# The mixer stage of a two-block transformer kernel: input norm applied after the projection, group norm taken in two halves, and the memory rows given a place of their own

## The reference, cut to what matters

```python
hn = _rmsnorm(x, norm_mix[l])                       # x: 256 x 1024
z = hn @ w_in[l]                                    # 1024 x 2560
x_lru, gate, q, k, v = jnp.split(z, splits, axis=-1)  # five parts of 512
y_a = _rg_lru(x_lru, conv_w, conv_b, ...) * jax.nn.gelu(gate)
y_b = _chunk_attention(q, k, v, rel_bias[l])        # 8 heads of 64, band mask and bias
y = jnp.concatenate([_rmsnorm(y_a, norm_grp_a[l]), _rmsnorm(y_b, norm_grp_b[l])], axis=-1)
x = x + y @ w_out[l]                                # 1024 x 1024
x = x + _memory_cross_attention(_rmsnorm(x, norm_cross[l]), _rmsnorm(mem, norm_mem[l]), ...)
```

## Time and profile before

| | us |
|---|---|
| median of 3 runs | 1633.67 (1632.15 to 1634.11) |
| the profiled execution | 1634.35 |
| its span, first to last instruction | 1632.6 |
| TensorE busy | 1527.7 (94%) |
| VectorE busy | 903.1 (55%) |
| ScalarE busy | 818.9 (50%) |
| GpSimd busy | 566.8 (35%) |

### The profile page before, as it was taken

How to read it: one execution, slowest core, us unless ns; L and a number is a source line. 1 busy time by engine, 2 the same in 40 slices (tenths; PEclk the granted TensorE clock), 3 DMA queues, 4 the chain that set the end, 5 groups by cost and what they waited for, 6 DMA issues and landing times.

```text
span 1632.6 us, 28309 instructions
## 1 busy us (share of the span) xinstructions
PE 1527.7 (94%) x10643; PEld 1407.4 (86%) x10643; DVE 903.1 (55%) x2131; ACT 818.9 (50%) x1437; POOL 566.8 (35%) x256
## 2 busy tenths in 40 slices
PE   6999999989979879898999889999999999999998
PEld 5998899978869779888999668999999999999886
DVE  6835348388342332132896996555555555555555
ACT  4546454488335724444455665444444444444444
POOL 5761655510456446726688991000000000000000
PEclk9999999999989979999999999999999999999999
DMA  6750334600233243424254004555554555555553
GB/s 258 278 173 36 142 117 168 220 27 2 101 106 129 78 155 130 155 109 146 81 198 140 1 0 180 181 181 188 191 184 180 181 188 191 184 180 182 176 195 129
DMA packets 37529, 238.47 MB, mean 146 GB/s; under 512 B 4160, under 2 KB 4288, under 8 KB 13248
## 3 DMA queue, kind: packets, MB, share of 16 engines
q1 hardware_dynamic: 37440, 237.27, 40.5%
HBM read 236.21 MB, written 1.05 MB: 145 GB/s over the span
## 4 chain that ended last, share of the span: by engine, by line
PE 64%; POOL 6%; DVE 4%; ACT 3%; issue 3%; DMA 1%; POOLq 0%; DVEq 0%; ACTq 0%; SPq 0%
PE bank L1058 21%; PE bank L639 15%; PE bank L642 7%; PE bank L722 6%; PE bank L725 4%; POOL raw L1117 3%; PE bank L825 2%; PE bank L682 2%; PE bank L843 2%; POOL wlo L1113 2%; PE bank L654 1%; POOL arena L1123 1%; ACT whi L1189 1%; PE bank L632 1%; PE bank L832 1%
## 5 line engine op out<-in xcount | busy, mean ns | idle before, releaser
L1113 POOL TENSOR_TENSOR wlo<-raw,whi 128x2048 fp32r<-128x2048 f32 x42 | 194.2, 4624 | 203.6 <-ACT whi L1189 203.6
L639 PE MATMUL bank<-hThi,whi 128*128 128x256 f32 x1024 | 250.4, 283 | 1.5 <-ACT whi L1489 1.5
L1113 POOL TENSOR_TENSOR wlo<-arena,whi 128x2048 fp32r<-128x2048 f32 x42 | 193.6, 4613 | 165.2 <-ACT whi L1189 165.2
L639 PE MATMUL bank<-hTlo,whi 128*128 128x256 f32 x1024 | 250.1, 282 | 0.0
L1058 PE MATMUL bank<-whi,ghi 128*128 128x512 f32 x512 | 203.1, 397 | 1.6 <-DVE glo L2170 0.5
L1058 PE MATMUL bank<-whi,glo 128*128 128x512 f32 x512 | 202.9, 396 | 0.0
L1058 PE MATMUL bank<-wlo,ghi 128*128 128x512 f32 x512 | 202.1, 395 | 0.0
L639 PEld LDWEIGHTS bank<-hThi,whi 128*128 128x128 f32 x1024 | 194.7, 190 | 6.0 <-ACT whi L1489 1.9
L639 PEld LDWEIGHTS bank<-hTlo,whi 128*128 128x128 f32 x1024 | 195.0, 190 | 4.1 <-issue 0.2
L1492 ACT ACTIVATE gact<-bank 128x256 f32<-128x256 f32 x96 | 37.0, 385 | 257.5 <-PE bank L642 257.5
L2165 DVE TENSOR_TENSOR gact<-gact,arena 128x256 f32<-128x256 f32 x96 | 40.8, 426 | 187.8 <-ACT gact L1492 187.8
(11 more groups left out here) (298 smaller groups left out, 3148.8 us busy)
## 6 DMA issues: line engine op xcount, KB each, us to landing
raw<-ex_in SPq DMA_DIRECT2D x64, 1024.0 KB, 4.7
raw<-w_in SPq DMA_DIRECT2D x44, 1024.0 KB, 4.8
arena<-w_in SPq DMA_DIRECT2D x44, 1024.0 KB, 4.8
xw<-ex_in SPq DMA_DIRECT2D x32, 1024.0 KB, 4.7
raw<-ex_in SPq DMA_DIRECT2D x54, 512.0 KB, 3.8
xw<-ex_in SPq DMA_DIRECT2D x10, 512.0 KB, 3.7
arena<-frt_in SPq DMA_DIRECT2D x1, 3904.0 KB, 15.1
arena<-tab_in SPq DMA_DIRECT2D x1, 1089.0 KB, 16.2
```

The source lines that it names most:

```text
L639: mm(out, lhs, rhs, start=(k == 0), stop=False)
L1113: G.tensor_tensor(wlo[:, u % 2, :], slots[u % RING], whi[:, u % 2, :], ALU.subtract).then_inc(lo_ready, 1)
```

## The change

- `mix_in` goes the newer way: x's pieces (`"mix"`, gain in, no row scale) are transposed inside `ple1`'s second chunk, and chunk c is a unit of pieces. The row scales, which are per token and thus lie along the columns, come as a row repeated on all partitions: ScalarE builds two diagonal matrices, TensorE multiplies a matrix of ones with them (`row_of_scales`), VectorE copies the row to `scale_row` and multiplies it in when it takes chunks c, c+2 and c+3 (`take_scaled`). The gate's chunk c+1 is scaled in PSUM by VectorE and then taken by ScalarE with its Gelu; v's chunk c+4 is taken by ScalarE with the token's scale.
- Chunk c is now "crossed" (both banks are done only with its second unit). The splits of the weights on ScalarE stand in another order among the recurrence's steps.
- y stays as it is, channels on the partitions. Its sum of squares is a product of its squares with a column of ones; its row of scales a second `row_of_scales`; VectorE multiplies it in during the attention, ScalarE rounds it to `hThi` and VectorE makes `hTlo`, all inside the attention's loop.
- The attention takes all eight heads of the first 128 tokens, then those of the second. Its half is normed alone (`half_rows`), the first tokens' squares inside the loop.
- The first chunk of `mix_out` (`by_halves`) begins with the 48 matmuls of y's channels, into banks 0, 1, 4 and 5; then come, for each half of the tokens, 4 transposes and 12 matmuls for each unit.
- The memory rows are loaded to `MEM`, once y is there, and normed before the splits for `mix_out`'s second chunk; that chunk multiplies whi with hTlo before wlo with hThi.

```diff
+SCALED = [first_of("mix_in") + i for i in (0, 2, 3)]
-PIECES = ["moba_o", "ple0", "norm1", "nsa_o", "ple1", "mem", "cross", "mem_o", "ffn"]
+PIECES = ["moba_o", "ple0", "norm1", "nsa_o", "ple1", "mix", "mem", "cross", "mem_o", "ffn"]
-CROSSED = {first_of(s) for s in ("mem_k", "mem_q", "query")}
+CROSSED = {first_of(s) for s in ("mix_in", "mem_k", "mem_q", "query")}
...
-                    sp_.wait_ge(tr_done, tr_all("grp"))
                     sp_.wait_ge(y_ready, 1)
-                    sp_.dma_start(OR, mem_d).then_inc(mem_loaded, 16)
+                    sp_.dma_start(MEM, mem_d).then_inc(mem_loaded, 16)
...
+                    if c == first_of("mix_out") + 1:
+                        parts = ((wh, hThi), (wh, hTlo), (wl, hThi))
...
-            ple(1, lambda: last_added("nsa_out", "ple1"))
-            transposes("mix")
-            activations("mix")
+            ple(1, lambda: last_added("nsa_out", "ple1"), "mix")
+            def row_of_scales(n, b):
+                pe.wait_ge(diag_ready, n)
+                for t in range(TT):
+                    last = mm(b[:, P * t:P * t + P], ones, diag[t], start=True, stop=True)
+                last.then_inc(row_done, 1)
...
-            project(c)
+            project(c, pieces=("mix", lambda: last_ple(1, "mix")))
+            pe.wait_ge(piece_lo[2], nth("mix"))
+            pe.wait_ge(ones_ready, 1)
+            row_of_scales(1, bank[6])
...
-            project(c + 4)
-            transposes("y")
+            def sums_of_y():
+                pe.wait_ge(ysq_ready, 1)
+                for t in range(TT):
+                    for b in range(4):
+                        last = mm(bank[4][:, t:t + 1], lb[:, b, P * t:P * t + P], ones[:, 0:1], start=(b == 0), stop=(b == 3))
+                last.then_inc(ysum_done, 1)
+            project(c + 4, sums_of_y)
+            pe.wait_ge(takenV, taken_before(c + 4, "V"))
+            row_of_scales(2, bank[0])
...
-            transposes("grp")
-            activations("grp")
+            def by_halves(c):
+                wh, wl = ([w[:, u, :].rearrange("p (k n) -> p k n", k=KT) for u in range(2)] for w in (whi, wlo))
+                def part(j, u, ks):
+                    for i, (w, h) in enumerate(((wh, hThi), (wl, hThi), (wh, hTlo))):
+                        for k in ks:
+                            last = mm(bank[(0, 1, 4, 5)[2 * j + u]][:, 0:UC], h[:, k, P * j:P * j + P], w[u][:, k, :],
+                                      start=(i == 0 and k == 0), stop=(i == 2 and k == KT - 1))
+                    return last
+                def heads(t):
+                    pe.wait_ge(half_rows, t + 1)
+                    for b in range(4):
+                        last = nc.tensor.transpose(bank[6 + t][:, P * b:P * b + P], OR[:, t, CW + P * b:CW + P * b + P], ident)
+                    last.then_inc(half_tr, 1)
+                def attended(j, u):
+                    pe.wait_ge(half_hi, j + 1)
+                    pe.wait_ge(half_lo, j + 1)
+                    return part(j, u, range(4, KT))
+                pe.wait_ge(y_lo, 1)
+                pe.wait_ge(lo_ready, split_before(2 * c) + 2)
+                pe.wait_ge(pt_ready, FIRST_JOB[2] + len(PHASES[2]))
+                for j in range(2):
+                    for u in range(2):
+                        part(j, u, range(4))
+                heads(0)
+                attended(0, 0)
+                heads(1)
+                attended(1, 0).then_inc(proj_done, 1)
+                attended(0, 1)
+                attended(1, 1).then_inc(proj_done, 1)
...
+                    if phase == 2 and i == 5:
+                        split()
+                    if phase == 2 and i == 6:
+                        act.wait_ge(yn_ready, 1)
+                        A(hThi[:, 0:4, :], la, ACT.Copy).then_inc(y_hi, 1)
+                    if phase == 2 and i == 14:
+                        act.wait_ge(o_taken, PHASES[2][7]["number"] + 1)
+                        A(gsq, OR[:, 0, CW:D], ACT.Square, accum_out=ss[:, 0:1])
...
+            act.wait_ge(scale_ready, 5)
+            diagonals()
             c = first_of("mix_in")
-            take(c)
-            take(c + 1, ACT.Gelu_apprx_tanh)
+            split_on(c)
+            for j in range(2):
+                split()
+                act.wait_ge(gg_scaled, j + 1)
+                A(gg[:, 2 * j:2 * j + 2, :], bank[2 * ((c + 1) % 2) + j][:, :].rearrange("p (b t) -> p b t", b=2),
+                  ACT.Gelu_apprx_tanh).then_inc(takenA, 1)
...
             gate(0)
-            take(c + 2)
-            gate(1)
             act.wait_ge(u_ready, 1)
...
+            split()
+            gate(1)
+            split()
             act.wait_ge(ix_ready, 1)
...
-            take(c + 4)
+            split()
+            act.wait_ge(y_ready, 1)
+            A(lb, la, ACT.Square).then_inc(ysq_ready, 1)
+            split()
+            split()
+            roots(2)
+            act.wait_ge(y_scale, 1)
+            diagonals()
+            A(sums[:, 8:10], x_scale, ACT.Exp, scale=-1.0)
+            take(c + 4, scale=x_scale, split_first=False)
             attention(2)
-            act.wait_ge(y_ready, 1)
-            squares(OR, 512, 2)
-            roots(4)
+            A(root[:, 4:6], rinv[:, 0:2], ACT.Sqrt)
+            act.wait_ge(o_taken, PHASES[2][-1]["number"] + 1)
+            A(gsq, OR[:, 1, CW:D], ACT.Square, accum_out=ss[:, 1:2]).then_inc(ss_ready, 1)
+            roots(2)
+            act.wait_ge(mem_loaded, 16)
+            squares(MEM, D)
+            roots(2)
             split_on(first_of("mix_out"))
-            act.wait_ge(mem_loaded, 16)
-            squares(OR, D)
-            roots(2)
...
+                    if phase == 2 and i in (2, 3):
+                        dve.wait_ge(row_done, 2)
+                        for b in (2 * i - 4, 2 * i - 3):
+                            last = V.scalar_tensor_tensor(la[:, b, :], la[:, b, :], sm("grp")[:, b:b + 1], bank[0][:, 0:T],
+                                                          ALU.mult, ALU.mult)
+                        if i == 3:
+                            last.then_inc(yn_ready, 1)
+                    if phase == 2 and i == 9:
+                        dve.wait_ge(y_hi, 1)
+                        V.tensor_tensor(hTlo[:, 0:4, :], la, hThi[:, 0:4, :], ALU.subtract).then_inc(y_lo, 1)
...
+            take_scaled(c + 3)
+            dve.wait_ge(ysum_done, 1)
+            rsqrt(2, 1.0 / 512, bank[4])
+            dve.sem_inc(y_scale, 1)
             attention(2)
-            dve.sem_inc(y_ready, 1)
-            row_norm(OR, OR, 512, 2)
-            take_transposed("grp")
-            row_norm(OR, OR, D, 1, piece_rows)
+            attended = OR[:, :, CW:D]
+            row_norm(attended, attended, 512, 1, half_rows)
...
+            row_norm(MEM, MEM, D, 1, piece_rows)
```

More of the change, by code:

```diff
@@ L167, in build @@
         sp = arena[:, at_tab + NTAB + NSML + NFRT:at_tab + NTAB + NSML + NFRT + 24].rearrange("p (a b) -> p a b", b=4)
+        spare = at_tab + NTAB + NSML + NFRT + 24
+        ones = arena[:, spare:spare + P]
+        diag = [arena[:, spare + P + P * t:spare + 2 * P + P * t] for t in range(TT)]
+        scale_row = arena[:, spare + 3 * P:spare + 3 * P + T]
         cosg = gact[:, 0, 0:64]
@@ L270, in groups_chunk @@
         def groups_chunk():
-            for h0 in range(0, 8, 4):
-                for t in range(TT):
+            for t in range(TT):
+                for h0 in range(0, 8, 4):
                     nk = P * (t + 1)
@@ L331, in destinations @@
                 if i == 0:
-                    return [xpad[:, 2 * j:2 * j + 2, 3:259] for j in range(2)]
+                    return [xpad[:, j:j + 3:2, 3:259] for j in range(2)]
                 dst = {1: gg, 2: QT, 3: KTb}[i]
@@ L422, in tr_cmp_k @@
                        odd=odd_nsa[4][:, 0:P].unsqueeze(1))
-        def tr_y():
-            for t in range(TT):
-                yield dict(blocks=[la[:, b, P * t:P * t + P] for b in range(4)],
-                           out=OR[:, t, 0:512].rearrange("p (b n) -> p b n", b=4), gain=None, rows=1)
         def tr_sel(t):
@@ L468, in nth @@
             return PIECES.index(name) + 1
-        FEEDS = dict(moba_o="moba_out", ple0="ple0", norm1="nsa_in", nsa_o="nsa_out", ple1="ple1", mem="mem_k",
+        FEEDS = dict(moba_o="moba_out", ple0="ple0", norm1="nsa_in", nsa_o="nsa_out", ple1="ple1", mix="mix_in", mem="mem_k",
                      cross="mem_q", mem_o="mem_o", ffn="query")
@@ L1989, in _ @@
             last.then_inc(xc_ready, 1)
+            for j in range(2):
+                z = projected(c + 1, j)
+                V.tensor_tensor(z, z, scales, ALU.mult).then_inc(gg_scaled, 1)
+            dve.wait_ge(frt_loaded, 16)
+            V.scalar_tensor_tensor(bias, bias, 1.0 / SCALE, tb("chunk_mask").unsqueeze(1).to_broadcast([P, 8, 256]),
+                                   ALU.mult, ALU.add).then_inc(bias_ready, 1)
             dve.wait_ge(ri_exp, 1)
```

100 lines of the change are left out of this document (67 added, 33 removed).

## The result

The changed kernel takes 1616.32 us (median of four; 1615.40 to 1617.68), the one before 1633.89 in the same rounds: ratio 0.9893, 95% interval 0.988 to 0.9906. Forecast were 1613.5 us and a range of 1607 to 1622. The profiled execution, at 1617.68 us the longest of the four, has a span of 1615.8 us for 1632.6, 16.8 less.

A forecast was written before the change was run, and what follows sets the result against it. TensorE was taken as the bound, so gains are its standstills and slow stretches. Minus 8.6 (attention's start), plus 3.4 (attention), minus 16.5 (behind it), plus 1.5 (clock) gave minus 20.2 us: 1613.5 us, range 1607 to 1622.

The forecast's parts named there:

- The pieces of x: Start of mix_in: with ple1 running as ple0 does, its first product comes at 471.4 instead of 485.12, 13.8 us earlier.
- Row of scales hidden: mix_in, behind chunk c: diagonals ready at 481.5, before TensorE asks at 484.5; the row costs TensorE about 0.3 us.
- Waits for low parts: mix_in: TensorE waits for the weights' low parts 2.4 us in unit 2c+2, 0.4 in 2c+6, 1.1 in 2c+7.
- Rival 1: mix_in: weights become the bound, each of nine units waiting 2.4 us; 17.7 us given back, 1631, likelier 1622; chance 0.15.
- y's sums: mix_in: eight one-column products for y's squares cost TensorE at most 0.9 us, at 0.11 each.
- A held step in y's root: Before the attention: a small VectorE TENSOR_SCALAR, held by GpSimd's subtraction, ends at 539.2, not 535.6; 2.5 us sooner if not held.
- Attention's start: The mixer's attention starts at 543.0 instead of 551.26, 8.3 us earlier, plus 0.3 for today's table wait.
- The table change: ScalarE before the attention: a table change costs 1.3 us, without the further drain of about 1.38 us the Trainium skill states.
- Rival 5: Attention's start: the longer table change, 2.66 us together as the Trainium skill has it, giving 1615; chance 0.03.
- The attention, +3.4: Mixer's attention: of 3.8 us inserted on ScalarE, plus VectorE work, it grows by 3.4 us, bounds 1 and 5.
- by_halves, 16.15 us without dips: mix_out's first chunk: y's products hide the norm, two waits of 2.1 us, 10.4 us less; 1.5 added for slow clock.
- Memory rows: mix_out's second chunk to mem_k: rows normed before anyone asks, transposes at full clock; 16.5 us saved from the attention's end on.

The follow-up runs named there:

- split_first: The changed kernel with the split of unit 2c+2 moved on ScalarE ahead of the wait for row scales and the first diagonals; 1614.49 us.
- root_in_psum: The changed kernel with y's root computed through PSUM, so that no VectorE operation of it has two SBUF inputs; 1614.07 us.
- weights_on_gpsimd: The changed kernel with the rounding of mix_out's second weight unit (2c+11) moved from ScalarE to GpSimd; 1613.88 us.
- both_on_gpsimd: The changed kernel with the rounding of weight unit 2c+11, y's rounding and y's low part all moved to GpSimd; 1612.73 us.
- combined_all: The changed kernel plus split_first, both_on_gpsimd, root_in_psum and by_halves' transposes issued behind earlier parts of y's products; 1604.02 us.
- split_later: The changed kernel with the split of unit 2c+10 moved behind y's second diagonals instead of ahead of y's root; 1613.95 us.
- memory_alone: The kernel before the change with only the memory rows' part: loaded into their own columns, squares ahead of mix_out's weight splits; 1630.14 us beside 1634.46.
- after_again: The changed kernel, unedited, timed again and profiled once more; 1617.32 us.

## Why the prediction was right, and by how much its steps were off

- *The pieces of x, -13.8 us at the first product.* Exact: 473.26, on the old clock 471.36, 471.4 said.
- *Row of scales hidden.* Right: L947 follows at once, chunk c+1 starts 0.36 us behind it.
- *Waits for low parts 2.4, 0.4, 1.1.* 2.00, about 0.4 and 1.16; split_first shows the cause of the first, the split queued behind the diagonals. Rival 1, that each unit waits, is refuted: chunk c+4 begins at 526.85 on the old clock, 526.8 said.
- *y's sums, at most 0.9 us.* Mis-sized by a factor of two. Eight products stand as 16 records and take 1.71 us (534.51 to 536.22). The 0.11 of a transpose is right for a record, but a product of f32 operands has two. The same count was hidden in the earlier trace rows, where 8 products of 256 columns are the 16 of L760, and in the gate's, whose eight records (1.54 us from 500.59 in after, L962) are four. For the row of scales the slip cost nothing: I said about 0.3, it is 0.36. Chunk c+4 ends 0.8 us late, at 540.15 on the old clock.
- *A held step in y's root.* The mechanism was right, shown by root_in_psum, the step not: I held only the TENSOR_SCALAR form of the earlier trace rows for one that waits, but the TENSOR_TENSOR on two SBUF columns waits as well and comes first. It ended at 539.5 on the old clock, 539.2 said. The Trainium skill ("SBUF — State Buffer", Who interferes with whom) states that a VectorE instruction with two SBUF inputs contends with a GpSimd instruction that reads SBUF, and one with at most one SBUF input outside the 2-port modes doesn't; the trace agrees on both, 4.37 us and 0.17. The price is of a wait, so it is bounded by what else is late: 1.95 us here, 2.5 in the prediction's range.
- *Attention's start, 543.0.* Measured 543.6 on the old clock. GpSimd ends 0.3 us later than said, two more short steps follow the held one (with the diagonals 0.2 more than said), v's take is 1.25 us for 1.1. The longer sums cost nothing here, since GpSimd's end, not theirs, releases the held step.
- *The table change.* Rival 5 is refuted again: the load of 1.28 at 542.79 is followed by the next activation at 544.08, 0.01 us behind its end. The drain of 1.38 us that the Trainium skill ("ScalarE: Activation LUTs", What ACT_TABLE_LOAD costs) states isn't there.
- *The attention, +3.4.* The weakest step, and mis-sized: +5.05, and 21.04 us where the prediction's own times (543.0 to 562.1) give 19.1. The prediction named a growth by over 5 us as a sign of being wrong. 5.05 is just over that line, and the nine executions with this attention show 4.67 to 5.80, seven of them over 5: by this sign the step was wrong, though the time lay in the range. I had let ScalarE's idle time take some of the 3.8 us inserted there, and gave VectorE's insertions no price. weights_on_gpsimd and both_on_gpsimd split it roughly: 1.74 for the split, 2.91 for y's rounding with its low part, 0.40 for squares, scaling, the new order of the heads and what clock is left. With the roundings gone and the clock at 1.00 the attention takes 16.06 us (combined_all), 0.07 more than before's 15.99, which has a table load of 1.28 inside. So the roundings are the cause, and next to nothing of their 4.2 us (1.89, 1.05 and 1.22) was hidden. The likely reason, argued and not tested by itself: each block of scores passes TensorE, VectorE and ScalarE in turn, and the idle time of each is the latency of the others. The half clock has a small share: 0.8 us between 0.71 and 0.92, 0.3 between 0.90 and 1.00 (both_on_gpsimd and combined_all).
- *by_halves, 16.15 us without dips, plus 1.5 for one.* 16.23 and 16.26 where there was none (root_in_psum, split_later); 19.17 in after with two, 17.63 with one. One dip was the right size; the profiled execution had one more.
- *Memory rows, the 6.1 us left of the 16.5 behind the 10.4.* Confirmed in memory_alone's trace, where they are 6.3; its median shows 4.3 (2.9 to 6.9).

The sum promised 20.2 us and the same account gives 16.1. Of the 4.1, 0.6 are the attention's start, 1.9 its length, 1.5 the second dip; the clock's luck behind `mem_k` gave 1.7 us back, which no step of the sum had counted. The median is 2.8 us above the forecast.

What I didn't see, though I wrote both waits of 2.1 us into the sum, is that they come from the order alone. Rows are scaled 3 us behind the attention's end. TensorE comes to their transposes at 571.62 in after, 5.1 us behind that end, and then stands while VectorE rounds. I priced the order as written and didn't ask which products could stand behind each group of transposes.

## What to carry to other kernels

When a producer hands over through a short VectorE step, put its transposes one block of independent products early; TensorE then works through the step. Work inserted into a loop whose blocks pass three engines in turn cost about its full length here, however idle each engine looked; try it on an engine that isn't in that ring. A small VectorE step on the critical path that would have two inputs in SBUF should have one in PSUM if GpSimd runs a long operation beside it: 0.17 us where it was held for 4.37.

## What the runs showed of the hardware

- GpSimd rounds 128x2048 f32 to fp32r in 1.89 us as CAST, and subtracts the same size in 4.53 to 4.62 (both_on_gpsimd, after).
- VectorE's RECIPROCAL from SBUF to SBUF isn't held by GpSimd's TENSOR_TENSOR (0.15 us beside it in root_in_psum, 0.17 in after); its TENSOR_TENSOR with two inputs in SBUF is (4.37 us in after), and not with one input in PSUM (0.16 and 0.17 in root_in_psum).
- A product of f32 operands stands as two records on TensorE, a transpose as one: from start to start, in after, a product takes 0.21 us for one column (8 in 1.71), 0.18 for 128 (2 in 0.36) and 0.39 for 256 (4 in 1.54, L962 from 500.59 to 502.13).
- One program shows the dips of TensorE's clock in different places: in `by_halves` after has them at 574 to 578 and again at 581 to 585, after_again at 574 to 578 alone; split_later, with the same `by_halves` and the same two waits of 2.04 us, has none.
